# The MLP's seven products per tile pair, added up in PSUM banks before they are read

## The chip, the cores and the metric

The kernel runs on one core of a Trainium2 chip. The metric is the device time of one execution in microseconds; smaller is better. The engines named below are TensorE (PE; its weight loads are a row of their own, PEld), VectorE (DVE), ScalarE (ACT), GpSimd (POOL) and SyncE (SP), which issues the DMAs.

## The reference

Two layers of a hybrid encoder over 1024 tokens of width 1024, in float32. Only the MLP of each layer matters here:

```python
hm = rms_norm(x, g_pre_mlp[i])
f = jnp.square(jax.nn.relu(hm @ w_mlp_up[i])) @ w_mlp_down[i]     # 1024 -> 4096 -> 1024
x = x + rms_norm(f, g_post_mlp[i])
```

Every float32 product is made from two rounded halves of each operand (high and low), as three matmuls that add up in one PSUM bank: high by high, high by low, low by high.

## The kernel before

**Tiles.** Activations lie with features on the 128 partitions and tokens along the free axis, in two halves of 512 tokens (t = 0, 1). An output of 128 features by 512 tokens fills one of the eight PSUM banks.

**Groups.** The hidden features are taken in 16 groups of 256. The first and the last are plain. The other 14 are done two at a time, in seven rounds per layer, counted by `G`; the text calls such a round a group. A group is 512 hidden features. On TensorE it is three hidden units (`big_unit(G, 1..3)`), the first unit of the next group, and then 28 `product(G, n)`. The seventh group of a layer has no next unit; after its products come the plain units of the end (`last_units`).

**Seven products.** In the down projection the 2 by 2 blocks of tokens (t), hidden features and outputs (`far`: output tile m or m + 4) are multiplied by a scheme with seven products in place of eight, called k = 1 to 7. Each product needs a sum or difference of weight blocks (made by GpSimd, line 2700 to 2711, or the plain block) and one of hidden blocks. A *turn* is one k for two output tiles (i = 0, 1 or 2, 3: a *pair*), that is two products, 12 matmuls, into two neighbouring banks. The 14 turns of a group stand in `TURNS` (line 130): first the seven of pair 0, then the seven of pair 2. `product` (1475) waits until the turn that last used its banks has been read.

**Parts.** `part.n` is the weight tile of product n. ScalarE copies it into the high half (line 1653, called by `big_part`), VectorE subtracts that from the source for the low half (2147, `big_part` at 2559). The halves go to a ring of seven places, so the copy of part n waits for product n - 7. The source lies in a raw buffer that SyncE loads by quarters (line 962); there are two raw buffers, so the load for output tile 2 waits for the low half of part.12, the load for tile 3 for that of part.13, and the next hidden unit (line 952) for that of part.26.

**Uses.** `use.u` is one VectorE instruction that adds two banks (128 partitions by 1024) onto the sum of outputs in SBUF, `facc` (2574). A product that belongs to two sums is read twice: `USES` lists 20 reads in a group. Four `whole` (2581) at a layer's end add two such sums together.

**Order.** Every engine works its instructions in a fixed order, written out by hand: `BIG_DVE` (273) and `BIG_ACT` (265) for the first six groups of a layer, `MLP_DVE` and `MLP_ACT` for the seventh and what follows. `unit.5` in them is the split of the second hidden unit of the next group into halves.

Of the kernel before, what the change touches and what calls it, by code (L numbers as in the profile page):

```python
# [46 lines left out]
BIG = (GROUPS - ENDS) // 2  # L47
QUARTERS = DC // 2
# [55 lines left out]
def rows_of(w):  # L104
# [5 lines left out]
    if w < PLE_AT:  # L110
# [16 lines left out]
PLAIN = [w for w in range(LOADS) if w not in QUARTERED]  # L127


TURNS = [(pair, k) for pair in (0, 2) for k in (1, 5, 2, 3, 6, 7, 4)]  # L130
PRODUCTS = [(pair + i, k) for pair, k in TURNS for i in range(2)]
MADE = len(PRODUCTS)
RING = 7
USES = {1: [(0, 0, 1), (1, 1, 1)], 2: [(0, 0, 1)], 3: [(0, 1, 1)], 4: [(1, 0, 1)],
        5: [(1, 0, -1), (1, 1, 1)], 6: [(1, 1, 1)], 7: [(0, 1, -1), (1, 1, 1)]}
USED = [(turn, t, far, sign) for turn, (pair, k) in enumerate(TURNS) for t, far, sign in USES[k]]
HIDDEN_ORDER = [(c, k) for c in range(2) for k in (1, 7, 4, 5, 6, 2, 3)]
SUM_ORDER = [(0, 5), (1, 5), (0, 7), (1, 7), (0, 6), (1, 6), (0, 4), (1, 4),
             (2, 5), (3, 5), (2, 7), (3, 7), (2, 6), (3, 6), (2, 4), (3, 4)]
# [3 lines left out]

def banks_of(G, turn):

    return (4, 6, 2, 0)[turn % 4]


def uses_until(turn):
# [124 lines left out]
hidden.0.1 sum.0.7 unit.2 hidden.0.7 value.1.1 hidden.0.4 sum.0.5 sum.0.6 hidden.0.5 hidden.0.6 value.1.0 hidden.0.2  # L274
sum.0.3 unit.3 hidden.0.3 value.2.1 part.0 value.2.0 hidden.1.1 sum.1.7 unit.4 hidden.1.7 value.3.1 hidden.1.4 sum.1.5
sum.1.6 hidden.1.5 hidden.1.6 part.1 part.2 part.3 part.4 part.5 part.6 value.3.0 hidden.1.2 sum.1.3 hidden.1.3
value.4.1 value.4.0 part.7 use.0 part.8 use.1 part.9 use.2 part.10 use.3 part.11 part.12 use.4 part.13 use.5
part.14 use.6 part.15 part.16 use.7 part.17 use.8 part.18 use.9 part.19 part.20 use.10 part.21 use.11 part.22
use.12 part.23 part.24 use.13 part.25 part.26 use.14 part.27 use.15 use.16 unit.5 use.17 use.18 use.19
""")  # L280

MLP_ACT = steps("""
# [24 lines left out]
group_sum.0.6 group_hidden.0.5 group_hidden.0.6 group_value.1.0 group_unit.3 group_hidden.0.2 group_sum.0.3  # L307
group_hidden.0.3 group_value.2.1 group_part.0 group_value.2.0 group_unit.4 group_hidden.1.1 group_sum.1.7
group_hidden.1.7 group_value.3.1 group_sum.1.5 group_part.1 group_hidden.1.4 group_hidden.1.5 group_sum.1.6
group_value.3.0 group_part.2 group_hidden.1.6 group_part.3 group_part.4 group_part.5 group_part.6 group_hidden.1.2  # L310
group_part.7 group_sum.1.3 group_part.8 group_part.9 group_part.10 group_hidden.1.3 group_part.11 group_use.0
group_part.12 group_use.1 group_use.2 group_part.13 group_use.3 group_use.4 group_part.14 group_use.5 group_use.6
group_part.15 group_part.16 group_use.7 group_use.8 group_part.17 group_part.18 group_part.19 group_part.20
group_use.9 whole.0 sum_down.0.1 group_part.21 group_part.22 group_part.23 group_part.24 group_part.25 group_use.10
group_part.26 sum_down.0.4 group_use.11 group_part.27 group_use.12 group_use.13 group_use.14 group_unit.5 group_use.15
group_use.16 group_use.17 group_use.18 group_use.19 sum_down.0.5 whole.1 sum_down.0.2 sum_down.0.3 whole.2
sum_down.0.6 sum_down.0.7 low.98 value.30.0 whole.3 rest.30.0 value.30.1 low.99 add_x.1.0.0 rest.30.1 add_x.1.0.1
add_x.1.0.2 value.31.0 sum_chunk.1.0.1 low.100 add_x.1.0.3 rest.31.0 low.101 value.31.1 low.102 low.103 rest.31.1
add_x.1.0.4 sum_chunk.1.0.2 sum_chunk.1.0.3 add.31.0 sum_chunk.1.0.4 add.31.1 add.31.2 add_x.1.0.5 add_x.1.0.6
add_x.1.0.7 sum_chunk.1.0.5 chunk.1.0.0 sum_chunk.1.0.6 add.31.3 sum_down.1.1 add.31.4 chunk.1.0.1 chunk.1.0.2 low.104  # L320
# [146 lines left out]
def encoder(nc, x_in, w_units, w_head, p_in, gains, table, consts, out):  # L467
# [17 lines left out]
    with ctx:  # L485
# [214 lines left out]
        big_sum = sem("big_sum")  # L700
        big_hi = sem("big_hi")
        big_lo = sem("big_lo")
        down_whole = sem("down_whole")
        part_sum = sem("part_sum")
        part_hi = sem("part_hi")
        part_lo = sem("part_lo")
# [423 lines left out]

        @block.tensor
        def _(pe):
            def split_product(dst, ah, al, bh, bl, start, stop):

                nc.tensor.matmul(dst, ah, bh, start=start, stop=False)  # L1135
                nc.tensor.matmul(dst, ah, bl, start=False, stop=False)  # L1136
                return nc.tensor.matmul(dst, al, bh, start=False, stop=stop)  # L1137

            def unit_output(bank, slot, t, ready=None, order=range(DC)):

# [74 lines left out]
            for L in range(DEPTH):  # L1215
# [259 lines left out]
                def product(G, n):  # L1475

                    i, k = PRODUCTS[n]
                    if i == 0:
                        pe.wait_ge(big_lo, max(hidden_at(L, G, c, o) for c in range(2) for o in (k, TURNS[0][1])))
                    pe.wait_ge(part_lo, made_at(L, G, n))  # L1480
                    turn = n // 2
                    bank = banks_of(G, turn)
                    if n % 2 == 0:
                        before = max([o for o in range(turn) if banks_of(G, o) == bank], default=None)
                        if before is not None:
                            pe.wait_ge(down_add, used_at(L, G, before))
                        elif bank < 4:
                            pe.wait_ge(up_v, up_at(L, G, 3, 0) if bank else up_at(L, G + 1, 0, 0) if G + 1 < BIG else up_at(L, G, 2, 0))
                        elif G:
                            pe.wait_ge(down_add, used_at(L, G - 1, max(o for o in range(len(TURNS)) if banks_of(G - 1, o) == bank)))  # L1490
                        else:
                            pe.wait_ge(down_copy, L * DC + DC)
                            pe.wait_ge(pre_ln, pre_at(L, 0) * 2 + 2)
                    r = made_at(0, G, n) - 1
                    for c in range(2):
                        tile = 2 * (r % RING) + c
                        at = (2 + tile // 8, tile % 8)
                        last = split_product(ps[:, bank + n % 2, :], wh[:, at[0], at[1], :], wl[:, at[0], at[1], :],
                                             hidden_part(c, k, 0), hidden_part(c, k, 1), c == 0, c == 1)
                    last.then_inc(down_out, 1)  # L1500

                def bank_of_lead(m):
# [143 lines left out]
        def _(act):  # L1646
# [115 lines left out]
            for L in range(DEPTH):  # L1762
# [294 lines left out]
                def down_square(t, m):  # L2057
                    if t:
                        act.wait_ge(down_add, L * ADDS + ADDS - DC + m + 1)
                    else:  # L2060
                        act.wait_ge(down_out, down_at(L, BIG - 1, PRODUCTS.index((QUARTERS - 1, 1))))
                        if m < QUARTERS:
                            act.wait_ge(down_add, used_at(L, BIG - 1, TURNS.index((m // 2 * 2, 2))))
                        else:
                            act.wait_ge(down_whole, L * 4 + (m - QUARTERS) // 2 + 1)
                    square((L, "post", 1, t, m), facc[:, t, m, :])

                def embedding(n):
# [73 lines left out]
        def _(dve):  # L2142
# [98 lines left out]
            for L in range(DEPTH):  # L2241
# [235 lines left out]
                def steps_of(order):  # L2477
                    for e in order:
                        if needless(L, e):
                            continue  # L2480
                        if e[0].startswith("group_"):
                            big_step(BIG - 1, e[0][6:], *e[1:])
                        elif e[0] == "low":
                            split_unit(L, e[1])
                        elif e[0] in ("post_low", "pre_low"):
                            low_of_total(L, e[0].split("_")[0], *e[1:])
                        elif e[0] == "add_x":
                            residual_chunk(L, *e[1:])
                        elif e[0] == "chunk":
                            pre_low(L, *e[1:])  # L2490
                        elif e[0] in ("sum_out", "sum_chunk", "sum_down", "sum_use"):
                            add_square(square_of(L, e))
                        elif e[0] == "value":
                            hidden_value(e[1], e[1] % 2, e[2], 0 if e[1] < 3 else 1)
                        elif e[0] == "rest":
                            hidden_rest(e[1], e[1] % 2, e[2])
                        elif e[0] == "add":
                            add_one(e[2])
                        elif e[0] == "whole":
                            whole(e[1])  # L2500
                        elif e[0] == "z":
                            gate_value(e[1])
                        elif e[0] == "y":
                            gated(e[1])
                        elif e[0] == "in":
                            in_first(L + 1, e[1])
# [13 lines left out]
                def add_one(m):  # L2520

                    dve.wait_ge(down_out, L * DOWNS + DOWNS - DC + m + 1)
                    if m < QUARTERS:
                        dve.wait_ge(down_whole, L * 4 + 3 + m // 2)
                    f = facc[:, 1, m, :]
                    V.tensor_tensor(f, f, ps[:, 4 + m % 3, :], ALU.add).then_inc(down_add, 1)

# [36 lines left out]

                def big_use(G, u):

                    turn, t, far, sign = USED[u]
                    dve.wait_ge(down_out, down_at(L, G, 2 * turn + 1))
                    before = max([o for o in range(u) if USED[o][1:3] == (t, far) and TURNS[USED[o][0]][0] == TURNS[turn][0]], default=None)
                    if before is not None:  # L2570
                        dve.wait_ge(down_add, L * ADDS + G * len(USED) + before + 1)
                    m, bank = TURNS[turn][0] + QUARTERS * far, banks_of(G, turn)
                    f = facc[:, t, m:m + 2, :]
                    V.tensor_tensor(f, f, ps[:, bank:bank + 2, :], ALU.add if sign > 0 else ALU.subtract).then_inc(down_add, 1)  # L2574

                def whole(n):

                    t, m = n // 2, 2 * (n % 2)
                    dve.wait_ge(down_add, used_at(L, BIG - 1, TURNS.index((m, 4 if t else 7))))
                    f = facc[:, t, m + QUARTERS * (1 - t):m + QUARTERS * (1 - t) + 2, :]  # L2580
                    V.tensor_tensor(f, f, facc[:, 1, m + QUARTERS:m + QUARTERS + 2, :], ALU.add).then_inc(down_whole, 1)

                def big_unit(G, j):
                    for w in units_of(G, j):
# [223 lines left out]
```

## Time and profile before

| what | value |
|---|---|
| median of three timed runs | 2713.61 us (2713.6 to 2713.67) |
| span of the profiled execution, first to last instruction | 2712.5 us |
| what lies around the span, by the median | 1.1 us |
| TensorE busy in the span | 2698.8 us, 99% |
| VectorE busy in the span | 2034.9 us, 75% |
| ScalarE busy, GpSimd busy | 1398.9 us, 302.7 us |

The page gives no time of the profiled execution apart from its span; the timed runs differ from one another by 0.07 us, so the median stands for it. Busy shares are means over stages: the attention, the MLP and the gates keep different engines busy. The end of a matmul in the trace is modelled, and matmuls overlap, so what tells TensorE's pace is the distance from one start to the next.

### The profile page before, as it was taken

How to read it: one execution, taken by the hardware profiler on the slowest of the kernel's cores; microseconds unless marked ns; L12 is line 12 of the kernel's file. 1: busy time of each engine (PE TensorE's matmuls, PEld its weight loads, DVE VectorE, ACT ScalarE, POOL GpSimd, SP SyncE). 2: the span in 40 equal slices, each digit the busy share in tenths (PEclk: the TensorE clock that was granted, in tenths of full speed). 3: DMA queues.
4: the chain of work that ended last, by engine and by line, in shares of the span. 5: the costliest groups of instructions: out<-in, count | busy, mean ns of one | idle time of the engine just before them, and what ended most of it. 6: DMA issues, size and time to landing. Idle time of an engine off the chain costs nothing.

```text
span 2712.5 us, 34671 instructions
## 1 busy us (share of the span) xinstructions
PE 2698.8 (99%) x12854; PEld 2242.9 (83%) x12854; DVE 2034.9 (75%) x2758; ACT 1398.9 (52%) x2401; POOL 302.7 (11%) x329
## 2 busy tenths in 40 slices
PE   9999999999999999999999999999999999999999
PEld 7888888888888888888888888888888888888886
DVE  5468888476787777798866788893867787777986
ACT  5337888564333333356634478884633333333464
POOL 0230000001111111110003200000011111111000
PEclk9999999999999999999999999999999999999999
DMA  4221112531111111133232111133311111111422
GB/s 166 78 72 37 34 34 76 181 109 71 62 47 55 39 58 51 63 117 117 86 119 73 60 41 34 29 132 131 140 45 49 63 47 55 39 55 55 148 94 78
DMA packets 85943, 206.19 MB, mean 76 GB/s; under 512 B 8976, under 2 KB 37776, under 8 KB 84752
## 3 DMA queue, kind: packets, MB, share of 16 engines
q1 hardware_dynamic: 85776, 203.97, 22.3%
q8 instruction: 103, 1.69, 0.3%
q14 instruction: 64, 0.52, 0.1%
HBM read 172.42 MB, written 31.52 MB: 75 GB/s over the span
## 4 chain that ended last, share of the span: by engine, by line
PE 96%; DVE 2%; ACT 1%; DMA 0%; issue 0%; SPq 0%; ACTq 0%
PE ps L1135 28%; PE ps L1137 28%; PE ps L1136 28%; PE ps L1344 4%; PE ps L1369 2%; PE ps L1368 2%; DVE nm L2386 1%; PE ps L1174 0%; PE ps L1175 0%; DVE ptl L2393 0%; PE ps L1309 0%; PE ps L1202 0%; ACT hh L1653 0%; DVE wl L2147 0%; PE ps L1160 0%; PE ps L1161 0%
## 5 line engine op out<-in xcount | busy, mean ns | idle before, releaser
L1135 PE MATMUL ps<-hh,wh 128*128 128x512 f32 x2160 | 847.9, 393 | 1.4 <-DVE hl L2183 1.3
L1137 PE MATMUL ps<-hh,wl 128*128 128x512 f32 x2160 | 840.8, 389 | 0.0
L1136 PE MATMUL ps<-hl,wh 128*128 128x512 f32 x2160 | 840.7, 389 | 0.0
L1653 ACT ACTIVATE wh<-raw 128x256 fp32r<-128x256 f32 (+2 forms) x510 | 319.2, 631 | 443.2 <-PE ps L1137 314.5
L2147 DVE TENSOR_TENSOR wl<-raw,wh 128x256 fp32r<-128x256 f32 (+2 forms) x510 | 379.6, 757 | 159.0 <-ACT wh L1653 158.6
L1135 PEld LDWEIGHTS ps<-hh,wh 128*128 128x128 f32 x2160 | 405.6, 188 | 89.1 <-issue 3.6
L1136 PEld LDWEIGHTS ps<-hl,wh 128*128 128x128 f32 x2160 | 405.6, 188 | 86.9 <-issue 3.6
L1137 PEld LDWEIGHTS ps<-hh,wl 128*128 128x128 f32 x2160 | 405.5, 188 | 84.5
L2574 DVE TENSOR_TENSOR xf<-xf,ps 128x1024 f32<-128x1024 f32 x280 | 337.4, 1214 | 35.9 <-PE ps L1137 34.7
L1135 PE MATMUL ps<-hx,wh 128*128 128x512 f32 x448 | 174.4, 389 | 0.5 <-DVE xf L2574 0.5
L1137 PE MATMUL ps<-hx,wl 128*128 128x512 f32 x448 | 174.3, 389 | 0.0
L1136 PE MATMUL ps<-hx,wh 128*128 128x512 f32 x448 | 174.3, 389 | 0.0
L2393 DVE TENSOR_TENSOR ptl<-ps,pth 128x512 fp32r<-128x512 f32 x256 | 163.8, 680 | 9.4 <-ACT pth L1653 8.8
L1653 ACT ACTIVATE pth<-ps 128x512 fp32r<-128x512 f32 x256 | 140.5, 595 | 48.2 <-PE ps L1344 45.0
L2386 DVE TENSOR_REDUCE nm<-ps 128x1 f32<-128x1024 f32 x128 | 155.4, 1214 | 1.4 <-PE ps L1137 1.1
L1865 ACT ACTIVATE pr<-ps,nm 128x1024 f32<-128x1024 f32 x128 | 142.8, 1115 | 14.2 <-DVE nm L2386 12.4
L2700 POOL TENSOR_TENSOR spare<-raw 128x256 f32<-128x256 f32 x56 | 43.2, 771 | 872.3 <-DMA raw<-w_units 872.3
L1344 PE MATMUL ps<-cst,pr 128*128 128x128 f32 x1024 | 138.3, 274 | 1.2 <-DVE ptl L2393 1.2
L1344 PEld LDWEIGHTS ps<-cst,pr 128*128 128x128 f32 x1024 | 116.2, 140 | 15.5 <-issue 4.0
L1368 PE MATMUL ps<-pth,vv 128*128 128x256 f32 x512 | 128.1, 284 | 0.0
L1369 PE MATMUL ps<-ptl,vv 128*128 128x256 f32 x512 | 127.2, 283 | 0.0
L1690 ACT ACTIVATE sq<-xf 128x512 f32<-128x512 f32 x168 | 103.1, 623 | 45.0 <-DVE accy L2177 19.8
(241 smaller groups left out, 4303.3 us busy)
## 6 DMA issues: line engine op xcount, KB each, us to landing
raw<-w_units SPq DMA_DIRECT2D x170, 512.0 KB, 3.4
raw<-w_units SPq DMA_DIRECT2D x112, 256.0 KB, 2.9
x_mid<-xf SPq DMA_DIRECT2D x4, 2048.0 KB, 7.9
xf<-x_mid SPq DMA_DIRECT2D x4, 2048.0 KB, 7.7
hh<-mix_hi SPq DMA_DIRECT2D x14, 512.0 KB, 6.1
hl<-mix_lo SPq DMA_DIRECT2D x14, 512.0 KB, 7.0
stage<-w_head SPq DMA_DIRECT2D x16, 320.0 KB, 3.3
mix_hi<-cyh SPq DMA_DIRECT2D x8, 512.0 KB, 2.6
```

The costliest lines, as they stand in the source:

```text
L1135: nc.tensor.matmul(dst, ah, bh, start=start, stop=False)
L1136: nc.tensor.matmul(dst, ah, bl, start=False, stop=False)
L1137: return nc.tensor.matmul(dst, al, bh, start=False, stop=stop)
L1344: last = nc.tensor.transpose(ps[:, 4 + b, c * P:(c + 1) * P], pr[:, s % 2, (4 * b + c) * P:(4 * b + c + 1) * P], ident)
L1368: nc.tensor.matmul(dst, vv[:, a, c, V_DIM:3 * V_DIM], pth[:, G % 2, c, :], start=c == 0, stop=False)
L1369: last = nc.tensor.matmul(dst, vv[:, a, c, 0:2 * V_DIM], ptl[:, G % 2, c, :], start=False, stop=c == 7)
L1653: return nc.scalar.activation(dst, src, ACT.Copy, **more)
L1865: nc.scalar.activation(pr[:, s % 2, :], ps[:, 2 * (s % 2):2 * (s % 2) + 2, :].rearrange("p b n -> p (b n)"), ACT.Exp, bias=nm[:, s % 2:s % ...
L2147: return V.tensor_tensor(dst, whole, high.bitcast(f32), ALU.subtract)
L2386: V.tensor_reduce(nm[:, s % 2:s % 2 + 1], ps[:, 2 * (s % 2):2 * (s % 2) + 2, :].rearrange("p b n -> p (b n)"), AX.X, ALU.min).then_inc(s_l ...
L2393: V.tensor_tensor(ptl[at], ps[:, 4 + b, :].rearrange("p (c q) -> p c q", c=4), pth[at].bitcast(f32), ALU.subtract).then_inc(t_lo, 1)
L2574: V.tensor_tensor(f, f, ps[:, bank:bank + 2, :], ALU.add if sign > 0 else ALU.subtract).then_inc(down_add, 1)
```

## The change

The order of the seven products in a pair becomes 1, 5, 6, 2, 7, 3, 4, and each product's two banks are given by the chain to which it belongs. A chain adds its products up in its banks without clearing them in between, and after each product the running sum is read once, as one whole contribution to one block of the output. So there are 14 uses in a group in place of 20, none with a subtraction, and no `whole`.

```diff
-TURNS = [(pair, k) for pair in (0, 2) for k in (1, 5, 2, 3, 6, 7, 4)]
+TURNS = [(pair, k) for pair in (0, 2) for k in (1, 5, 6, 2, 7, 3, 4)]
...
-USES = {1: [(0, 0, 1), (1, 1, 1)], 2: [(0, 0, 1)], 3: [(0, 1, 1)], 4: [(1, 0, 1)],
-        5: [(1, 0, -1), (1, 1, 1)], 6: [(1, 1, 1)], 7: [(0, 1, -1), (1, 1, 1)]}
-USED = [(turn, t, far, sign) for turn, (pair, k) in enumerate(TURNS) for t, far, sign in USES[k]]
+CHAINS = ((1, 6, 7, 4), (5, 3), (2,))
+USES = {1: (0, 0), 6: (0, 1), 7: (1, 1), 4: (1, 0), 5: (1, 1), 3: (0, 1), 2: (0, 0)}
+USED = [(turn,) + USES[k] for turn, (pair, k) in enumerate(TURNS)]
...
 def banks_of(G, turn):
-    return (4, 6, 2, 0)[turn % 4]
+    pair, k = TURNS[turn]
+    chain = next(i for i, row in enumerate(CHAINS) if k in row)
+    return ((4, 6, 2), (0, 6, 2))[pair // 2][chain]
+
+
+def chain_starts(k):
+    return any(row[0] == k for row in CHAINS)
...
-value.4.1 value.4.0 part.7 use.0 part.8 use.1 part.9 use.2 part.10 use.3 part.11 part.12 use.4 part.13 use.5
-part.14 use.6 part.15 part.16 use.7 part.17 use.8 part.18 use.9 part.19 part.20 use.10 part.21 use.11 part.22
-use.12 part.23 part.24 use.13 part.25 part.26 use.14 part.27 use.15 use.16 unit.5 use.17 use.18 use.19
+value.4.1 value.4.0 use.0 part.7 part.8 part.9 part.10 use.1 part.11 use.2 part.12 part.13 part.14 use.3 part.15
+use.4 part.16 part.17 part.18 use.5 part.19 part.20 use.6 part.21 use.7 part.22 part.23 part.24 use.8 part.25 use.9
+part.26 part.27 use.10 unit.5 use.11 use.12 use.13
...
                         last = split_product(ps[:, bank + n % 2, :], wh[:, at[0], at[1], :], wl[:, at[0], at[1], :],
-                                             hidden_part(c, k, 0), hidden_part(c, k, 1), c == 0, c == 1)
+                                             hidden_part(c, k, 0), hidden_part(c, k, 1),
+                                             chain_starts(k) and c == 0, c == 1, not chain_starts(k))
```

`MLP_DVE` is changed in the same way: in the seventh group use.0 to use.2 now stand ahead of part.12 (before, use.0 alone), use.3 stands behind part.14, use.4 behind part.15, unit.5 ahead of use.11, use.13 behind use.12 and two `sum_down`, and the four `whole` are gone. Waits on `whole` become waits on the uses that complete a block. ScalarE's, GpSimd's and SyncE's orders are unchanged; they take their tiles by product number, so they follow the new order of k.

## Rows read from the trace of the kernel before

**Rows 1.** The page: engines' busy time, and the group of the uses.
```profile
PE 2698.8 (99%) x12854; PEld 2242.9 (83%) x12854; DVE 2034.9 (75%) x2758; ACT 1398.9 (52%) x2401; POOL 302.7 (11%) x329
...
L2574 DVE TENSOR_TENSOR xf<-xf,ps 128x1024 f32<-128x1024 f32 x280 | 337.4, 1214 | 35.9 <-PE ps L1137 34.7
```

**Rows 2.** Waits of TensorE in the whole span: total us, times, longest.
```profile
PE ps L1135 <- DVE xf L2574: 0.5, 2, 0.2
```

**Rows 3.** Busy time by stretch, layer one's seven groups; last columns granted clock, DMA.
```profile
677.00:1196.00 519.00, 518.76 (x2289) 429.22 (x2289) 400.46 (x537) 184.11 (x351) 86.57 (x104) 1.00 0.17 54
```

**Rows 4.** Timeline of PE, fifth group: first matmuls of turns 0, 6, 13.
```profile
1003.91 0.39 PE L1135 MATMUL ps<-hz,wh 128*128 128x512 f32 x1
...
1020.23 0.39 PE L1135 MATMUL ps<-hx,wh 128*128 128x512 f32 x1
...
1039.27 0.39 PE L1135 MATMUL ps<-hx,wh 128*128 128x512 f32 x1
```

**Rows 5.** Timeline of PE and DVE, a stretch in which DVE waits.
```profile
1141.95 0.39 PE L1135 MATMUL ps<-hh,wh 128*128 128x512 f32 x1
...
1144.67 0.39 PE L1135 MATMUL ps<-hh,wh 128*128 128x512 f32 x1
...
1145.55 0.69 DVE L2533 SCALAR_TENSOR_TENSOR stage<-ps,rpre 128x512 f32<-128x512 f32 x1 [3.31 <-PE ps L1137]
```

**Rows 6.** Timeline of DVE, fifth group: parts 11 to 13, 15, 16; two uses.
```profile
1012.37 0.84 DVE L2147 TENSOR_TENSOR wl<-raw,wh 128x256 fp32r<-128x256 f32 x2
1013.13 1.21 DVE L2574 TENSOR_TENSOR xf<-xf,ps 128x1024 f32<-128x1024 f32 x1
1014.26 0.42 DVE L2147 TENSOR_TENSOR wl<-raw,wh 128x256 fp32r<-128x256 f32 x1
...
1019.44 0.62 DVE L2147 TENSOR_TENSOR wl<-raw,wh 128x256 fp32r<-128x256 f32 x1 [0.51 <-ACT wh L1653]
1019.98 0.96 DVE L2147 TENSOR_TENSOR wl<-spare,wh 128x256 fp32r<-128x256 f32 x1
...
1036.75 1.22 DVE L2574 TENSOR_TENSOR xf<-xf,ps 128x1024 f32<-128x1024 f32 x1 [1.50 <-PE ps L1137]
```

**Rows 7.** Timeline of ACT and SP, fifth group: parts 14, 15; quarters' loads.
```profile
1016.62 0.42 ACT L1653 ACTIVATE wh<-raw 128x256 fp32r<-128x256 f32 x1 [2.51 <-DMA raw<-w_units]
1018.99 0.42 ACT L1653 ACTIVATE wh<-raw 128x256 fp32r<-128x256 f32 x1 [1.95 <-DMA raw<-w_units]
...
1013.24 2.35 SPq L962 DMA_DIRECT2D raw<-w_units  x4
```

**Rows 8.** Timeline of DVE and PE, seventh group: PE waits for a use.
```profile
1185.19 1.21 DVE L2574 TENSOR_TENSOR xf<-xf,ps 128x1024 f32<-128x1024 f32 x1
...
1185.93 0.39 PE L1137 MATMUL ps<-hy,wl 128*128 128x512 f32 x1
1186.55 0.47 PE L1135 MATMUL ps<-hx,wh 128*128 128x512 f32 x1 [0.24 <-DVE xf L2574]
1186.86 0.39 PE L1136 MATMUL ps<-hx,wh 128*128 128x512 f32 x1
```

**Rows 9.** Timeline of SP and ACT: load and copy of unit.5, fourth, fifth group.
```profile
950.93 6.94 SPq L952 DMA_DIRECT2D raw<-w_units  x3
...
954.40 1.06 ACT L1653 ACTIVATE wh<-raw 128x1024 fp32r<-128x1024 f32 x1 [2.85 <-DMA raw<-w_units]
...
1032.53 7.73 SPq L952 DMA_DIRECT2D raw<-w_units  x3
...
1037.59 1.06 ACT L1653 ACTIVATE wh<-raw 128x1024 fp32r<-128x1024 f32 x1 [4.43 <-DMA raw<-w_units]
```

**Rows 10.** Timeline of ACT and PE, seventh group: part 15, turn 6, the end.
```profile
1171.68 0.42 ACT L1653 ACTIVATE wh<-raw 128x256 fp32r<-128x256 f32 x1 [2.14 <-DMA raw<-w_units]
...
1172.55 0.39 PE L1135 MATMUL ps<-hx,wh 128*128 128x512 f32 x1
...
1194.83 0.39 PE L1135 MATMUL ps<-hh,wh 128*128 128x512 f32 x1
```

More of the change, by code:

```diff
@@ L309 @@
 group_hidden.1.7 group_value.3.1 group_sum.1.5 group_part.1 group_hidden.1.4 group_hidden.1.5 group_sum.1.6
[L310 to L317, printed above, removed]
+group_value.3.0 group_part.2 group_hidden.1.6 group_part.3 group_part.4 group_part.5 group_part.6 group_use.0
+group_hidden.1.2 group_part.7 group_part.8 group_sum.1.3 group_part.9 group_part.10 group_use.1 group_part.11 group_use.2
+group_hidden.1.3 group_part.12 group_part.13 group_part.14 group_use.3 group_part.15 group_use.4 group_part.16
+group_part.17 group_part.18 group_use.5 group_part.19 group_part.20 group_use.6 group_part.21 group_use.7 group_part.22
+group_part.23 group_part.24 group_use.8 sum_down.0.1 group_part.25 group_use.9 group_part.26 sum_down.0.4 group_part.27
+group_use.10 sum_down.0.5 group_unit.5 group_use.11 sum_down.0.2 sum_down.0.3 group_use.12 group_use.13 sum_down.0.6
+sum_down.0.7 low.98 value.30.0 rest.30.0 value.30.1 low.99 add_x.1.0.0 rest.30.1 add_x.1.0.1
 add_x.1.0.2 value.31.0 sum_chunk.1.0.1 low.100 add_x.1.0.3 rest.31.0 low.101 value.31.1 low.102 low.103 rest.31.1
@@ L702, in encoder @@
         big_lo = sem("big_lo")
-        down_whole = sem("down_whole")
         part_sum = sem("part_sum")
@@ L1132, in _, with split_product @@
         def _(pe):
[L1133 to L1137, printed above, removed]
+            def split_product(dst, ah, al, bh, bl, start, stop, joins=False):
+                nc.tensor.matmul(dst, ah, bh, start=start, stop=False, skip_group_check=joins)
+                nc.tensor.matmul(dst, ah, bl, start=False, stop=False, skip_group_check=joins)
+                return nc.tensor.matmul(dst, al, bh, start=False, stop=stop, skip_group_check=joins)
             def unit_output(bank, slot, t, ready=None, order=range(DC)):
@@ L2061, in down_square @@
                         act.wait_ge(down_out, down_at(L, BIG - 1, PRODUCTS.index((QUARTERS - 1, 1))))
[L2062 to L2065, printed above, removed]
+                        act.wait_ge(down_add, used_at(L, BIG - 1, TURNS.index((m % QUARTERS // 2 * 2, 2 if m < QUARTERS else 3))))
                     square((L, "post", 1, t, m), facc[:, t, m, :])
@@ L2498, in steps_of @@
                             add_one(e[2])
-                        elif e[0] == "whole":
-                            whole(e[1])
                         elif e[0] == "z":
@@ L2522, in add_one @@
                     dve.wait_ge(down_out, L * DOWNS + DOWNS - DC + m + 1)
-                    if m < QUARTERS:
-                        dve.wait_ge(down_whole, L * 4 + 3 + m // 2)
+                    dve.wait_ge(down_add, used_at(L, BIG - 1, TURNS.index((m % QUARTERS // 2 * 2, 4 if m < QUARTERS else 7))))
                     f = facc[:, 1, m, :]
@@ L2565, in big_use @@
                 def big_use(G, u):
-                    turn, t, far, sign = USED[u]
+                    turn, t, far = USED[u]
                     dve.wait_ge(down_out, down_at(L, G, 2 * turn + 1))
@@ L2573, in big_use @@
                     f = facc[:, t, m:m + 2, :]
[L2574 to L2581, printed above, removed]
+                    V.tensor_tensor(f, f, ps[:, bank:bank + 2, :], ALU.add).then_inc(down_add, 1)
                 def big_unit(G, j):
```

## The prediction

> **What bounds the kernel.** I read the page first: TensorE is busy for 2698.8 of 2712.5 us, VectorE for 75% [rows 1]. A share over stages does not say what the changed stage is worth, so next came TensorE's waits over the whole span. For the uses, the instructions that the change thins out, it waits 0.5 us in two places, all there is [rows 2]. Then the stretch of the change alone: in the 519 us of a layer's seven groups TensorE stands idle for 0.24 us while VectorE works 400.46, and the granted clock is 1.00 [rows 3]. Here TensorE is the bound, and nothing that VectorE saves can shorten the stretch by more than that idle time and its small after-effect.
>
> The timeline of TensorE gives the beat. From the first matmul of turn 0 to the first of turn 13 are 13 turns of 12 matmuls in 35.36 us [rows 4]: 2.72 us a turn, 0.2267 a matmul. The beat is the same in a stretch in which VectorE sat idle, 12 matmuls in 2.72 us [rows 5], so fewer reads of PSUM do not make matmuls faster. A group is 360 matmuls, 81.6 us.
>
> **What is removed.** 84 uses (6 in each of 14 groups) and 8 `whole`, 1.21 us each [rows 1], about 110 us of VectorE. All of it lies under TensorE's work, so it is costed at nothing: TensorE waited for it for 0.24 us a layer, which with the slow restart described next is 0.47. That much is gained twice. The matmuls are as many as before, of the same form; whether the first of a product clears its bank or adds to it I cost at nothing, since the three matmuls of a split product, one of which may clear, follow one another on one beat.
>
> **What is added: a dependence between products.** Before, four pairs of banks went round, and a turn's banks came back four turns later, so a read could be some 6 us late unnoticed (three turns, less the read). After, turns 0, 2, 4, 6 of a pair use the same banks, and turns 1 and 5 too. Turn 6 may not start before the sum of turn 4 has been read, one turn of 2.72 us after turn 4 ended. A read on time fits: it starts 0.20 us after the next turn's first matmul would (1036.75 against 1003.91 + 12 x 2.72 = 1036.55) [rows 4, 6], lasts 1.21, and leaves 1.3 us. A late one costs more than its lateness. In the one place where TensorE waited for a use, the read ended at 1186.40, the next matmul was due at 1186.16, so it was 0.24 late; the matmul behind it came at 1186.86 instead of 1186.39, a loss of 0.47 [rows 8]. I charge lateness plus 0.23.
>
> VectorE works in a fixed order, so a read is late when what stands ahead of it waits. I went through the new order with the times of the fifth group. Turns 2, 4, 9 and 11 find their reads on time: ahead of use.0, use.2, use.7 and use.9 stand only parts whose ring place came free a product earlier. Two do not.
>
> *Turn 6 waits for use.4, which stands behind part.15.* Part.15's copy waits for the load of the second quarter: 1018.99. The low half follows at 1019.44, the next instruction 0.54 later [rows 6, 7]. So use.4 starts at 1019.98 at the earliest and ends at 1021.19. Turn 6 is due at 1020.23 [rows 4]: 0.96 late, 1.19 lost. Also the load itself moves. The first quarter was asked for at 1013.24, when part.12 was done (1012.37 + 0.84) [rows 6, 7]. Now use.2 stands ahead of part.12: it can start at 1012.27 (turn 3's due time 1012.07 + 0.20), holds the queue 1.13 (1013.13 to 1014.26), part.12 ends 0.42 after that, 1013.82: 0.61 later. Whether the second quarter, which is asked for behind part.13 as before, moves too, no row shows. If not, the loss is 1.19; if it queues fully behind the first, 1.80. The quarters' copies lie 2.37 us apart [rows 7] though four issues took SyncE 2.35, so they share the transfer; I take two thirds of the shift: 1.6 us. Twelve groups have this order: 12 x 1.6 = 19.2 us. Who waits besides: part.16 and the rest stand behind use.4, but their products are three turns away.
>
> *Turn 13 waits for use.11, which stands behind unit.5.* The next unit's load waits for part.26, which now stands behind use.9. In the fourth group (81.6 earlier, turn 10 due at 949.51) use.9 starts at 949.71, part.26 at 950.84, done at 951.26, load asked for at 951.3 where it was 950.93. From there to the copy took 3.47 us [rows 9]: copy at 954.77, done 955.83, low half 955.86, use.11 956.99 (1.13, like a use of the same size), read over at 958.20. Turn 13 is due at 957.67: 0.53 late, 0.76 lost. In the fifth group the load took 5.06 [rows 9], and the loss is 2.35. Of the twelve groups ten are like the first and two like the second: 7.6 + 4.7 = 12.3 us. Before, unit.5 stood one turn further back, and what came behind it was not due.
>
> *The seventh group of each layer.* Two more uses stand ahead of part.12, on a VectorE that has no gap there: 2.3 us later (2 x 1.13). Part.15's copy was at 1171.68, turn 6 due at 1172.55 [rows 10]. Copy, low half, use add 0.45 + 0.54 + 1.21 = 2.20, so unmoved the loss is 1.33 + 0.23 = 1.56; moved in full, 3.86; by two thirds, 3.1. Turn 13 as above, 0.76. And the plain unit that follows the products is written to banks 0 and 1, now those of turn 13 itself: due at 1194.83 [rows 10], it has to wait for use.13, 0.20 + 1.21 later: 1.41 + 0.23 = 1.64. Together 5.5, less the 0.47 of today: 5.0, twice, 10.1 us. Behind that point VectorE has less to do than before, and TensorE waited for nothing there [rows 2], so nothing comes back.
>
> *GpSimd.* Its order is the same, but k = 6 is wanted four parts earlier. In the first pair this puts parts 4 and 5 behind two more of its sums, before the products start; in the second, parts 18 and 19, several us ahead of their products. I cost it at nothing; with that cover gone, it is the last rival.
>
> **Sum.** 19.2 + 12.3 + 10.1 = 41.6 us. Added to the profiled execution, span 2712.5 and 1.1 around it, which is the median of 2713.6: 2755.2 us. With every unknown at its low end (1.19 and 0.76 in all twelve groups; 1.56 in the seventh): 14.3 + 9.1 + 7.0 = 30.4, 2744. At the high end (1.80; two more slow loads; 3.86): 21.6 + 15.5 + 11.6 = 48.7, 2762.
>
> A rule speaks about this change. The Trainium skill, Perfetto Trace Analysis, section Matmuls, says that independent groups of matmuls should go round different PSUM banks so that the reading of one lies under the matmuls of the next. Taken alone it is met by one turn in other banks between two products of a chain, and would give the time of the first rival. The rows show that a read fits, and also that the queue ahead of it does not: by them the rule is met in six re-entries of a group and not in two.
>
> **Rivals.** *Not slower.* The re-entries are hidden: loads land early enough. For turn 6 the copy of part.15 would have to come 1.0 us sooner than 1018.99, for turn 13 unit.5's 0.53 sooner; the queue orders make both loads later, not sooner. Left is the end of the layer, 2 x (1.64 - 0.47): 2716, within 0.2%, which is about what a measurement of this kernel tells from no change. Chance 0.05. *Faster* would need shorter matmuls, since the idle time to be won is 0.9 us; the equal beat in rows 5 speaks against it. 2712.7 or, with shorter matmuls, under 2708: chance 0.02. *One of the two re-entries is hidden*, most likely turn 6 by quicker quarters: 41.6 - 19.2 - 2 x 3.1 = 16.2, 2730. Chance 0.09. *More re-entries are late*: once TensorE has waited, parts that GpSimd feeds hold up a further use. Two more of 0.6 in each of twelve groups: 14.4, 2770. Against it, five us of cover. Chance 0.09. The forecast has 0.75.
>
> **How the numbers follow.** Predicted 2755. The range 2734 to 2772 takes in the forecast's own 2744 to 2762, most of the last two rivals' spread and leaves about 2 in 10 outside. Slower by over 0.2%: 0.75 + 0.09 + 0.09 = 0.93; within: 0.05; faster: 0.02.
>
> **What the profile after would show.** VectorE's busy time down by some 110 us; 196 uses. TensorE with waits for uses (line of `big_use`) of some 20 to 35 us in all and restarts beside them; in each group one wait ahead of turn 6 of 1 to 2 us, behind a part whose copy waited for a load, and one ahead of turn 13, behind a 128 x 1024 low half; one at the first plain unit. The beat between remains 0.2267. The prediction is wrong if those waits are missing, if they stand at other turns, or if the loads of quarters and units land at other distances from their issue than above.

## The result, and the profile after

The change makes the kernel slower: 2767.57 us (median of four runs, 2764.5 to 2768.82) against 2713.64 us of before in the same comparison, a ratio of 1.0198, 95% interval 1.0184 to 1.0211. The profiled execution took 2768.2 us, its span 2766.4. The direction was as predicted and the time lies inside the range of 2734 to 2772, but above the 2744 to 2762 that the sum itself allowed.

The page after: engines' busy time, then the group of the uses and the group of the products' matmuls that wait (busy, mean ns | idle before, and what ended it).

```profile
PE 2710.1 (98%) x12854; PEld 2243.4 (81%) x12854; DVE 1931.8 (70%) x2666; ACT 1401.0 (51%) x2401; POOL 298.8 (11%) x329
...
L2573 DVE TENSOR_TENSOR xf<-xf,ps 128x1024 f32<-128x1024 f32 x196 | 237.2, 1215 | 66.6 <-PE ps L1141 66.5
L1139 PE MATMUL ps<-hx,wh 128*128 128x512 f32 x448 | 179.2, 400 | 39.2 <-DVE xf L2573 39.1
```

VectorE did lose its work: 84 uses fewer, 2034.9 us down to 1931.8 [rows 1]. TensorE has the same 12854 matmuls and a lower share. The waits of TensorE by cause say why (total us, times, longest):

```profile
PE ps L1139 <- DVE xf L2573: 41.9, 30, 3.3
```

Two waits of 0.5 us together [rows 2] have become 30 of 41.9. They are not spread about: in the timeline they stand at turn 6 and at turn 13 of each of the 14 groups, and at the first plain unit behind each layer's products. 2 x 14 + 2 = 30. The fifth group of layer 1, turn 6, on SP, ACT, DVE and PE:

```profile
1024.55 1.91 SPq L966 DMA_DIRECT2D raw<-w_units  x4
...
1030.17 0.42 ACT L1658 ACTIVATE wh<-raw 128x256 fp32r<-128x256 f32 x1 [1.60 <-DMA raw<-w_units]
...
1030.62 0.62 DVE L2149 TENSOR_TENSOR wl<-raw,wh 128x256 fp32r<-128x256 f32 x1 [0.27 <-ACT wh L1658]
1031.16 1.21 DVE L2573 TENSOR_TENSOR xf<-xf,ps 128x1024 f32<-128x1024 f32 x1
...
1030.70 0.39 PE L1141 MATMUL ps<-hy,wl 128*128 128x512 f32 x1
1032.51 0.47 PE L1139 MATMUL ps<-hx,wh 128*128 128x512 f32 x1 [1.43 <-DVE xf L2573]
```

Read it from the end. TensorE stands for 1.43 us until use.4 is done (1031.16 + 1.21). Use.4 follows at once on the low half of part.15 (1030.62), which waited for ScalarE's copy (1030.17), which waited for the second quarter's load. Turn 6 was due at 1030.93 (1030.70 and a beat), so the sum that use.4 reads was there a turn earlier: the read could have begun at 1028.4 (1030.93 - 2.72 + 0.20). The same group, turn 13, on ACT, DVE and PE:

```profile
1049.95 1.06 ACT L1658 ACTIVATE wh<-raw 128x1024 fp32r<-128x1024 f32 x1 [4.40 <-DMA raw<-w_units]
...
1051.05 1.23 DVE L2149 TENSOR_TENSOR wl<-raw,wh 128x1024 fp32r<-128x1024 f32 x1 [3.40 <-ACT wh L1658]
1052.19 2.35 DVE L2573 TENSOR_TENSOR xf<-xf,ps 128x1024 f32<-128x1024 f32 x2
...
1053.55 0.47 PE L1139 MATMUL ps<-hx,wh 128*128 128x512 f32 x1 [1.72 <-DVE xf L2573]
```

Here the load is the next unit's, and use.11 (the first of the two uses in the third row) stands behind unit.5.

One thing stands beside the waits. After the longest one of the twelve full groups (a layer's first six groups are called full here) the matmuls come back slowly; timeline of PE, and the same stretch by windows (the column before the last two is the granted clock):

```profile
2315.78 0.39 PE L1141 MATMUL ps<-hy,wl 128*128 128x512 f32 x1
2318.84 0.77 PE L1139 MATMUL ps<-hx,wh 128*128 128x512 f32 x1 [2.67 <-DVE xf L2573]
2319.40 0.63 PE L1140 MATMUL ps<-hx,wh 128*128 128x512 f32 x1
2319.83 0.63 PE L1141 MATMUL ps<-hx,wl 128*128 128x512 f32 x1
...
2322.27 0.40 PE L1141 MATMUL ps<-hx,wl 128*128 128x512 f32 x1
2322.50 0.39 PE L1139 MATMUL ps<-hx,wh 128*128 128x512 f32 x1
```
```profile
2315.00:2327.00 12.00, 9.33 (x35) 7.33 (x34) 9.94 (x13) 3.23 (x8) 5.46 (x8) 0.86 0.02 7
```

From 2319.40 to 2319.83 is 0.43 us, where the beat is 0.2267: the lower of the clock's two levels, 1.2 GHz in place of 2.4, for seven matmuls. Below, *slow restart* means this return at the lower clock, and *re-entry* what every wait costs beside its length (the 0.23 us that the prediction calls a slow restart). The Trainium skill, TensorE: Matmul & The Clock Gate, section HAM oscillation — how this bites in real kernels, warns that waiting for data can put the clock down so that the work behind the wait starts slow; the trace agrees, with a clock of 0.86 over these 12 us, though the page's wait is one for a DMA and this one is for a read.

**Where the time went, wait by wait.** For each wait I took the start of the matmul six before it and of the twentieth after it, and subtracted 26 beats (where the next wait falls into that stretch, its loss is taken off again). Of the 30 waits 27 lose their length and 0.23 to 0.30 us. The other three (2.67, 2.88, 3.29 us) lose 1.75 to 1.80 beyond their length, some 1.5 us more each, by the slow restart.

| place | waits, us | lost by measurement | predicted |
|---|---|---|---|
| turn 6, 12 full groups | 18.7 | 23.3 | 19.2 |
| turn 13, 12 full groups | 11.3 | 14.4 | 12.3 |
| seventh groups, 3 waits each | 11.9 | 16.4 | 11.0 |
| gone: two waits of before | | -1.0 | -0.9 |
| sum | | 53.1 | 41.6 |

The span grew by 2766.4 - 2712.5 = 53.9 us. The waits account for it within 0.8.

### The profile page after: what moved, and what is told of

The parts are those of the page before. It is cut to its first block, busy times and chain, and to the rows that moved or that the text cites. A ratio compares the mean times of both kernels' runs of the same rounds, so it can differ in the third digit from the quotient of the medians.

```text
span 2766.4 us, 34503 instructions
## 1 busy us (share of the span) xinstructions
PE 2710.1 (98%) x12854; PEld 2243.4 (81%) x12854; DVE 1931.8 (70%) x2666; ACT 1401.0 (51%) x2401; POOL 298.8 (11%) x329
## 4 chain that ended last, share of the span: by engine, by line
PE 86%; DVE 6%; DMA 4%; ACT 2%; issue 1%; SPq 1%; POOL 0%; DVEq 0%; ACTq 0%; POOLq 0%
PE ps L1139 25%; PE ps L1141 25%; PE ps L1140 25%; DMA raw<-w_units 4%; PE ps L1348 4%; DVE xf L2573 3%; PE ps L1373 2%; PE ps L1372 2%; DVE wl L2149 1%; ACT wh L1658 1%; DVE nm L2388 1%; SPq L966 0%; PE ps L1178 0%; PE ps L1179 0%; DVE ptl L2395 0%
## 5 line engine op out<-in xcount | busy, mean ns | idle before, releaser
L2149 DVE TENSOR_TENSOR wl<-raw,wh 128x256 fp32r<-128x256 f32 (+2 forms) x510 | 373.2, 738 | 280.7 <-ACT wh L1658 280.0
L2573 DVE TENSOR_TENSOR xf<-xf,ps 128x1024 f32<-128x1024 f32 x196 | 237.2, 1215 | 66.6 <-PE ps L1141 66.5
L1139 PE MATMUL ps<-hx,wh 128*128 128x512 f32 x448 | 179.2, 400 | 39.2 <-DVE xf L2573 39.1
L1140 PE MATMUL ps<-hx,wh 128*128 128x512 f32 x448 | 176.0, 393 | 0.0
L1870 ACT ACTIVATE pr<-ps,nm 128x1024 f32<-128x1024 f32 x128 | 142.8, 1116 | 14.2 <-DVE nm L2388 12.3
L1139 PEld LDWEIGHTS ps<-hx,wh 128*128 128x128 f32 x448 | 85.2, 190 | 68.4 <-issue 51.7
L1348 PEld LDWEIGHTS ps<-cst,pr 128*128 128x128 f32 x1024 | 116.4, 140 | 14.4 <-issue 3.0
```

Source lines behind the costliest of these rows:

```text
L1139: nc.tensor.matmul(dst, ah, bh, start=start, stop=False, skip_group_check=joins)
L1140: nc.tensor.matmul(dst, ah, bl, start=False, stop=False, skip_group_check=joins)
L1348: last = nc.tensor.transpose(ps[:, 4 + b, c * P:(c + 1) * P], pr[:, s % 2, (4 * b + c) * P:(4 * b + c + 1) * P], ident)
L1870: nc.scalar.activation(pr[:, s % 2, :], ps[:, 2 * (s % 2):2 * (s % 2) + 2, :].rearrange("p b n -> p (b n)"), ACT.Exp, bias=nm[:, s % 2:s % ...
L2149: return V.tensor_tensor(dst, whole, high.bitcast(f32), ALU.subtract)
L2573: V.tensor_tensor(f, f, ps[:, bank:bank + 2, :], ALU.add).then_inc(down_add, 1)
```

## The experiments

Theory: all added time is TensorE waiting for a read that VectorE could have made in time, had it not stood in the written order behind work that waits for a load; the chains themselves cost nothing. Rival: sums in few banks, product on product, are slow in themselves. The edits are to the order of VectorE after the change, unless said otherwise. In all ratios the base is the kernel before, timed again with each run (medians of 2713.76 to 2714.45 us).

### Use.3 and use.4 ahead of parts 14 and 15

```diff
-... part.12 part.13 part.14 use.3 part.15 use.4 part.16 ...
+... part.12 part.13 use.3 use.4 part.14 part.15 part.16 ...
```

> VectorE's written order in the six full groups of each layer now has use.3 and use.4 ahead of parts 14 and 15; nothing else changes. Theory (the added time is waits for a PSUM read that stands in VectorE's order behind work waiting for weights): the twelve waits of turn 6, 1.03 to 2.67 us in the trace of after, 18.7 us in all and 0.23 us of re-entry each (21.5 us), go, and with them the one half-clock restart of that turn; the waits of turn 13 stay. 2767.6 - 21.5 - 1.5 = about 2744 to 2746 us, and the trace shows 18 waits for the read on L2573 in place of 30. Rival 1 (the chains themselves are slower, by dependent accumulation or by three banks being too few): the waits at turn 6 stay or move to a neighbouring turn, 2765 us or more. Rival 2 (parts 14 and 15 become late and hold up the weights of the next quarter): the turn-6 waits go but others as long come a quarter later, 2755 to 2768 us.

Measured: 2747.21 us, ratio 1.0122 (1.0107 to 1.0137), 20.4 us less than after the change. Use.4 and part.14 on DVE in the fifth group, and the first matmul of turn 6:

```profile
1022.03 1.22 DVE L2573 TENSOR_TENSOR xf<-xf,ps 128x1024 f32<-128x1024 f32 x1 [1.50 <-PE ps L1141]
1023.17 0.42 DVE L2149 TENSOR_TENSOR wl<-raw,wh 128x256 fp32r<-128x256 f32 x1
...
1024.55 0.39 PE L1139 MATMUL ps<-hx,wh 128*128 128x512 f32 x1
```

VectorE now waits for TensorE (1.50 us) and no longer TensorE for VectorE: all twelve waits of turn 6 are gone. Of 22 that remain, 12 are those of turn 13, six the seventh groups', and four new ones of 0.22 to 0.27 us stand at turn 9 of the second layer. These four lose 2.2 us with their re-entries. The median lies 1.2 us above the 2744 to 2746 expected; whether the four waits are the reason is not shown, since the profiled execution has them and took 2745.63 us. Turn 9 comes up again below.

### Use.11 ahead of unit.5

```diff
-... use.10 unit.5 use.11 use.12 use.13
+... use.10 use.11 unit.5 use.12 use.13
```

> VectorE's written order in the six full groups of each layer has use.11 ahead of unit.5; nothing else changes. Theory (the read is late because unit.5 waits for its own load): the twelve waits of turn 13, 0.44 to 1.84 us in the trace of after, 11.3 us in all and 0.23 us of re-entry each (14.1 us), go; those of turn 6 stay: 2767.6 - 14.1 = about 2753.5 us (2752 to 2755). Rival 1 (the chains or the number of banks are the cost): no change, 2766 to 2769 us. Rival 2 (unit.5, now 1.2 us later, is late for the turns that use it): the gain is lost again at the next group's first turns, 2762 us or more, with waits for unit.5's tile in the trace.

Measured: 2753.57 us, ratio 1.0145 (1.013 to 1.016), 14.0 us less, as expected. The waits of TensorE for uses:

```profile
PE ps L1139 <- DVE xf L2573: 30.9, 19, 2.9
```

The twelve waits of turn 13 are gone and those of turn 6 have stayed; with six in the seventh groups that makes 18. One of 0.22 us is new, at turn 2 of the second layer's seventh group. No wait for unit.5's tile has come up.

### Part.12 ahead of use.2: the load asked for earlier

```diff
-... part.11 use.2 part.12 part.13 ...
+... part.11 part.12 use.2 part.13 ...
```

> VectorE's written order has part.12 ahead of use.2, so that the load of the second quarter, which follows the buffer that part.12 frees, is asked for earlier; use.4 stays behind part.15. Theory: the turn-6 waits are as long as that load is late, so they get shorter by what the load is asked for earlier, 0 to 0.6 us each and not to nothing: 2760 to 2767.6 us, most likely 2763; use.2, 0.6 us later, still ends before its bank is wanted, and no wait comes in turn 4. Rival (any read made later by half a microsecond costs, since three banks leave no slack): new waits of about 0.3 us or more in turn 4 of each of twelve groups, 2768 to 2775 us.

Measured: 2759.71 us, ratio 1.0168 (1.0151 to 1.0185), 7.9 us less.

```profile
PE ps L1139 <- DVE xf L2573: 33.9, 30, 2.6
```

There are still 30 waits, and none at turn 4. The twelve of turn 6 sum to 12.4 us in place of 18.7. In the fifth group of layer 1 the first quarter's load is asked for 0.61 us earlier, counted from turn 0, as it was meant to be; the waits are 0.52 shorter on average, group by group 0.12 to 1.22. So the wait follows the load, but the loads themselves vary by more than the shift. With the slow restart of 2318.84 gone as well, the time lies just under the range expected.

### The new order of the products alone

The kernel before, with its banks and its one to two reads a product, in the order 1, 5, 6, 2, 7, 3, 4.

```diff
-TURNS = [(pair, k) for pair in (0, 2) for k in (1, 5, 2, 3, 6, 7, 4)]
+TURNS = [(pair, k) for pair in (0, 2) for k in (1, 5, 6, 2, 7, 3, 4)]
```

The wait of `whole` on the last use of a block is adapted to the new order as well.

> The kernel before with the new order of the seven products alone (1, 5, 6, 2, 7, 3, 4); its reads, its banks and its one to two reads a product stay as they were. Theory: the order of the products costs nothing, since both factors of each product are ready long before its turn: 2713.6 us, within 1 us of before, and waits for reads as before. Rival (the time is lost because the new order asks for tiles that GpSimd's sums deliver too late): clearly slower, 2720 us or more, with waits of TensorE for those tiles and not for PSUM reads.

Measured: 2716.16 us, ratio 1.0006 (0.9997 to 1.0016), no difference that can be told, though the median lies 1.7 us above its base and 1 was expected. "Waits for reads as before" did not quite hold either:

```profile
PE ps L1135 <- DVE xf L2574: 1.6, 4, 0.6
```

Two waits of 0.54 and 0.58 us have joined the two of before, one in each seventh group. With the old banks, the order is not the cause of the 54 us.

### Both moves, and then the banks at a layer's end

The first kernel has use.3, use.4 and use.11 moved ahead in all seven groups. The second exchanges two banks in the last group of a layer as well.

```diff
-    return ((4, 6, 2), (0, 6, 2))[pair // 2][chain]
+    return ((4, 6, 2), (2, 6, 0) if G == BIG - 1 else (0, 6, 2))[pair // 2][chain]
```

> use.3 and use.4 stand ahead of parts 14 and 15 and use.11 ahead of unit.5, in all seven groups of each layer; the three chains, their order and their banks stay as in the change. Theory (the added time is reads queued behind work that waits for weights, and the end of each layer): the 24 waits of turns 6 and 13 in the full groups go, and with them the wait of the seventh group's turn 6; what stays is the two waits at the end of each layer, 1.35 to 1.55 us each. 2713.6 + 2 x (2.8 + 0.5) = about 2719 us at most, 2716 where one of the two goes with the other (2715 to 2720). Rival (chains of dependent accumulation, or three banks in place of seven, cost time in themselves): clearly slower, 2730 us or more, with waits spread over other turns.

> As the kernel with use.3, use.4 and use.11 put ahead in all groups, and in the last group of each layer banks 0 and 2 are exchanged between the chains of the second pair, so that the bank that the next layer's or the end's products want first is not the one read last. Theory: the waits at the end of each layer go as well; what is left is the kernel before less the 2 x 0.47 us that it waited for reads: 2712.7 us, 2712 to 2714. Rival (the end of the layer is set by the last read itself, not by its bank): as the kernel without the exchange, 2715 to 2720 us.

Measured: 2722.37 us, ratio 1.0031 (1.0019 to 1.0044), and 2718.89 us, ratio 1.0019 (1.001 to 1.0027). The exchange is worth 3.5 us, about what the two waits at the layers' ends lose without it (1.70 and 2.19), but both kernels end some 3 to 6 us above what I expected. What is left in the second one, first by cause and then at the first place of the first layer's seventh group, on ACT, DVE and PE:

```profile
PE ps L1139 <- DVE xf L2573: 2.3, 7, 0.4
```
```profile
1177.83 0.42 ACT L1658 ACTIVATE wh<-raw 128x256 fp32r<-128x256 f32 x1 [2.22 <-POOL raw L2699]
...
1175.36 1.84 DVE L2149 TENSOR_TENSOR wl<-spare,wh 128x256 fp32r<-128x256 f32 x2
1178.28 0.50 DVE L2149 TENSOR_TENSOR wl<-raw,wh 128x256 fp32r<-128x256 f32 x1 [1.08 <-ACT wh L1658]
1178.70 1.21 DVE L2573 TENSOR_TENSOR xf<-xf,ps 128x1024 f32<-128x1024 f32 x1
...
1180.05 0.47 PE L1139 MATMUL ps<-hx,wh 128*128 128x512 f32 x1 [0.43 <-DVE xf L2573]
```

Part.18 (1178.28) waits 1.08 us for a copy (1177.83) whose source GpSimd (POOL) makes, and use.5 stands behind it. Turn 8, which takes use.5's banks, waits; turn 9 waits for use.7 for the same delay. It is the same fault a third time. After the change no wait stands there; as I read it, TensorE held up at turn 6 came to turn 8 that much later. Seven waits of 2.3 us in all and 0.26 more each make 4.1.

### Use.5 ahead of part.18 too

```diff
-... part.16 part.17 part.18 use.5 ...
+... part.16 part.17 use.5 part.18 ...
```

> The kernel with use.3, use.4 and use.11 put ahead and the banks exchanged at the end of a layer, and use.5 ahead of part.18 too. That kernel's trace has seven waits left for reads, 0.28 to 0.43 us, at turns 7 and 8, where use.5 stands behind part.18, whose source comes from GpSimd's sums; with what follows them they make 3 to 5 us. Theory (those are the last of the added time, and the chains cost nothing by themselves): no wait for a read is left, 2713 to 2714.5 us, the time of before within 1 us, though VectorE has 100 us less to do. Rival 1 (the chains cost a few us beside the waits): 2717 us or more again. Rival 2 (VectorE's saved work is worth something once the waits are gone): below 2711 us.

(Counted from zero, as elsewhere, the turns in this text are 8 and 9.) Measured: 2713.83 us against 2713.8 of before, ratio 1.0001 (0.9992 to 1.001). The page's busy times and the wait for uses:

```profile
PE 2698.7 (100%) x12854; PEld 2242.9 (83%) x12854; DVE 1933.2 (71%) x2666; ACT 1398.9 (52%) x2401; POOL 300.0 (11%) x329
```
```profile
PE ps L1139 <- DVE xf L2573: 0.6, 2, 0.4
```

Three chains, three pairs of banks in use at a time, 14 reads, and TensorE's busy time is that of before to 0.1 us [rows 1]. The chains cost nothing. VectorE does 102 us less, and that too is worth nothing. "No wait is left" was too much: two remain, as in before.

### Use.4 later still

```diff
-... part.15 use.4 part.16 part.17 part.18 ...
+... part.15 part.16 part.17 use.4 part.18 ...
```

> The change with use.4 put still later in VectorE's order, behind parts 16 and 17 (two subtractions that take 1.84 us together) in the six full groups of each layer; nothing else. The theory so far has two terms: a wait costs its length and about 0.26 us, and after the longest waits (2.67 us and more in the trace of the change, three of them) TensorE comes back at half its clock, which costs about 1.5 us more. The twelve waits of turn 6 become 1.84 us longer each, 2.9 to 4.5 us. By the length alone: 2767.6 + 12 x 1.84 = 2789.7 us, with the mean clock as it was, 0.998. With a half-clock restart behind each of the eleven that did not have one: 11 x 1.5 = 16.5 us more, 2806 us (2800 to 2810), a mean clock below 0.995, and matmuls at a pitch of 0.43 us behind these waits. Rival (VectorE catches up elsewhere, so that what is added in turn 6 is taken from the wait of turn 13): 2775 to 2785 us.

Measured: 2804.4 us, ratio 1.0338 (1.0321 to 1.0354), 36.8 us more than after the change. The twelve waits of turn 6 sum to 38.7 us, 1.67 more each, so length alone would give 2788. The mean clock is 0.990, and behind nine of the twelve TensorE comes back slowly: by the measure above, the twelve lose 62.0 us in place of 23.3. Two of them, timeline of PE, and their stretches by windows:

```profile
783.92 0.77 PE L1139 MATMUL ps<-hx,wh 128*128 128x512 f32 x1 [3.27 <-DVE xf L2573]
784.48 0.63 PE L1140 MATMUL ps<-hx,wh 128*128 128x512 f32 x1
...
2263.08 0.47 PE L1139 MATMUL ps<-hx,wh 128*128 128x512 f32 x1 [3.27 <-DVE xf L2573]
2263.39 0.39 PE L1140 MATMUL ps<-hx,wh 128*128 128x512 f32 x1
```
```profile
780.00:792.00 12.00, 8.73 (x26) 6.64 (x25) 7.34 (x10) 2.66 (x7) 4.65 (x6) 0.72 0.00 1
2259.00:2271.00 12.00, 8.73 (x39) 6.97 (x38) 9.22 (x13) 3.65 (x9) 5.50 (x7) 1.00 0.00 0
```

A wait therefore has a second price, which a sum of lengths does not hold.

## Why the prediction was right, and where its sum was short

**TensorE is the bound and VectorE's saving is worth nothing: shown.** The last repaired kernel has the saving and the time of before.

**Lateness plus 0.23 for a wait: right.** 0.23 to 0.31 was measured over all the runs behind waits without a slow restart.

**Turn 6 behind part.15, and by what: shown** by the move of use.4. Predicted 1.6 us a group, measured 1.94 (23.3 / 12), above my high end of 1.80. The mean wait was 1.56 us where I had 1.37. The step that was too small is "two thirds of the shift": asking 0.61 earlier won 0.52 on average, so most of the shift seems to reach the second quarter. One slow restart (1.5 us) is in the rest.

**Turn 13 behind unit.5: shown** by the move of use.11. The sum was near, 14.4 against 12.3, the pattern was not. "Ten are like the first and two like the second" came from two loads; the waits lie between 0.44 and 1.84 us all the way.

**The seventh groups.** Turn 6 was to be 2.87 us late (3.1 less 0.23): it waited 2.88 and 3.29, and a slow restart followed both. Turn 13 was taken as in the other groups, 0.76; it lost 1.6 and 1.8. ScalarE's squares stand ahead of the copies of parts 25 to 27 there, which I had not stepped through. With use.11 ahead of unit.5 there too, no wait of turn 13 is left; that the squares make unit.5 so late was read and not tried. The layer's end, 1.64, measured 1.70: the exchange of banks shows its cause.

**Where the sum was short.** By the table it was short by 11.5 us. 6.3 of them are length: the waits sum to 41.9 us, against some 35.6 in my terms and 20 to 35 in what I wrote of the profile after. Most of that is in three terms: turn 6 (2.3) and turn 13 (1.8) of the full groups, and turn 13 of the seventh (1.8). Another 4.5 are a term that I left out. I read a granted clock of 1.00 [rows 3] and held it for the time after; the change itself made waits after which that did not hold, three slow restarts. So the mechanism was right and the sizes were not, and the price of a wait as its length and a constant was incomplete.

**Luck.** 2767.57 us lies outside the sum's own 2744 to 2762. The range held because it had been widened to 2772 for *More re-entries are late*, a rival that did not happen.

**The rivals.** GpSimd's parts do hold up a use, but only where the other waits are repaired; in the change itself no such wait is seen, so the last rival was wrong as the account of 2767.6. *Not slower* exists as a kernel, with four reads moved and two banks exchanged. One turn of 2.72 us between two products of a chain is enough for a read of 1.21, if the read is not queued behind something that waits for a load.

## What to carry to other kernels

When a buffer comes back sooner, list for each reader what stands ahead of it in its engine's order, and ask of each whether it waits for a load: the reader inherits that wait. Put the reads that free a buffer ahead of work that waits for data, and do it again after each repair, since the next late one shows only then. Saved work on an engine that is not the bound buys nothing, and the slack that was paid for it can cost: price each new wait on TensorE by its length, about a quarter of a microsecond, and, as a risk, the slow restart. In these runs it followed 20 of the 27 waits for a use that were longer than 2 us, at some 1.5 to 3 us each, and none of the shorter ones.

## What the runs showed that was not expected

Whether TensorE comes back at 1.2 or 2.4 GHz is not told by the wait's length alone. Two waits of 3.27 us in one execution, at the same turn of two groups, differ: behind the one the clock is 0.72 over 12 us, and the wait loses 3.1 us beyond its length; behind the other it is 1.00, and the wait loses 0.25. With part.12 moved, a wait of 2.30 us was followed by a slow restart, and one of 2.26 was not; with use.4 later still, one of 2.07 was, and one of 2.96 was not. What decides between them was not tried and stays open.
